# Modulation chunks laid out by outputs and summed by VectorE's accumulator, with the S5 sets respaced

## What is computed

```python
c_act = jax.nn.silu(c)
for layer in range(2):
    mod = (c_act @ ada_w[layer] + ada_b[layer])[:, None, :]      # 6 x 1024 outputs
    shift_m, scale_m, gate_m, shift_f, scale_f, gate_f = jnp.split(mod, 6, axis=-1)
    h = _rmsnorm(x, norm_g[layer, 0]) * (1.0 + scale_m) + shift_m
    mix = _mixer_conv_retention(h, ...) if layer == 0 else _mixer_s5(h, ...)
    x = x + gate_m * mix
    h = _rmsnorm(x, norm_g[layer, 1]) * (1.0 + scale_f) + shift_f
    x = x + gate_f * (jnp.square(jax.nn.relu(h @ w_fc1[layer])) @ w_fc2[layer])
x = _rmsnorm(x, norm_f)
```

## Time and profile before

| | us |
|---|---|
| median of 3 runs | 1222.62 (1221.12 to 1224.0) |
| profiled execution, its own time | 1223.91 |
| its span, first to last instruction | 1222.1 |
| busy: TensorE / VectorE / ACT / POOL | 1181.8 / 856.5 / 531.9 / 434.5 |
| mean granted TensorE clock | 0.989 of full |

### The profile page before, as it was taken

How to read it: one execution, slowest core, us unless ns; L and a number is a source line. 1 busy time by engine, 2 the same in 40 slices (tenths; PEclk the granted TensorE clock), 3 DMA queues, 4 the chain that set the end, 5 groups by cost and what they waited for, 6 DMA issues and landing times.

```text
span 1222.1 us, 24460 instructions
## 1 busy us (share of the span) xinstructions
PE 1181.8 (97%) x10684; PEld 1113.0 (91%) x10684; DVE 856.5 (70%) x953; ACT 531.9 (44%) x675; POOL 434.5 (36%) x575
## 2 busy tenths in 40 slices
PE   6899999999999987999999999999999999999998
PEld 5786788999899977999999999898889999999998
DVE  5699898877679489847896343758885566666633
ACT  2130243543234254436454333466488535444331
POOL 7999689999989526400000001000000031000000
PEclk9899999999999999999999999999999999999999
DMA  9982777988887565374655455444333454545541
GB/s 346 395 329 104 243 257 263 360 301 324 324 313 269 213 234 194 119 256 152 233 181 188 159 205 181 160 143 145 132 136 129 151 182 164 195 154 203 190 159 66
DMA packets 112122, 258.18 MB, mean 211 GB/s; under 512 B 5120, under 2 KB 8848, under 8 KB 111888
## 3 DMA queue, kind: packets, MB, share of 16 engines
q1 hardware_dynamic: 83056, 196.18, 45.1%
q10 hardware_dynamic: 25504, 46.81, 10.8%
q0 software_dynamic: 3456, 13.63, 2.9%
HBM read 241.93 MB, written 14.68 MB: 210 GB/s over the span
## 4 chain that ended last, share of the span: by engine, by line
PE 69%; POOL 15%; issue 2%; DVE 1%; ACT 0%; DMA 0%; DVEq 0%; POOLq 0%
PE bank L1987 69%; POOL tabw L741 6%; POOL tabw L738 3%; POOL prep L746 3%; POOL tabw L746 1%; POOL tabw L777 1%; POOL tabw L779 0%; DMA prep<-in_s_bc 0%; POOL tabw L758 0%; PE bank L2560 0%; POOL s_wout L794 0%; DVE h_in L1408 0%; POOL memory_kv L774 0%; ACT prep L1076 0%; ACT ada_slot_split L919 0%
## 5 line engine op out<-in xcount | busy, mean ns | idle before, releaser
L1987 PE MATMUL bank<-squares_split,ring_split 128*128 128x256 f32 x1056 | 299.4, 284 | 0.0
L1987 PEld LDWEIGHTS bank<-squares_split,ring_split 128*128 128x128 f32 x1056 | 203.4, 193 | 0.0
L1380 DVE SCALAR_TENSOR_TENSOR ada_acc<-ada_slot,cact,ada_acc 128x512 f32<-128x512 f32 x150 | 134.8, 899 | 5.1
L1987 PE MATMUL bank<-ada_slot_split,ring_split 128*128 128x256 f32 x432 | 122.3, 283 | 0.0
L1432 DVE TENSOR_TENSOR ring_split<-ring,ada_slot_split 128x2048 fp32r<-128x2048 f32 (+1 forms) x31 | 70.1, 2264 | 55.8 <-ACT ada_slot_split L919 55.8
L1987 PE MATMUL bank<-big_split,ring_split 128*128 128x256 f32 x352 | 99.5, 283 | 0.0
L831 POOL TENSOR_TENSOR y_cat<-y_cat,tmp 128x512 f32<-128x512 f32 x8 | 10.7, 1339 | 235.8 <-DVE tmp L1891 235.8
L817 POOL TENSOR_TENSOR squares<-squares 128x512 f32<-128x512 f32 x4 | 5.5, 1384 | 240.7 <-ACT squares L1137 194.5
L1987 PE MATMUL bank<-big_split,ada_slot_split 128*128 128x256 f32 x296 | 84.9, 287 | 0.0
L1987 PEld LDWEIGHTS bank<-ada_slot_split,ring_split 128*128 128x128 f32 x432 | 82.9, 192 | 0.0
L1432 DVE TENSOR_TENSOR ring_split<-ring,tabw_split 128x2048 fp32r<-128x2048 f32 x22 | 50.4, 2291 | 41.3 <-ACT tabw_split L919 41.3
(11 more groups left out here) (440 smaller groups left out, 3865.6 us busy)
## 6 DMA issues: line engine op xcount, KB each, us to landing
ring<-in_w_fc SPq DMA_DIRECT2D x32, 2048.0 KB, 8.8
ada_slot<-in_ada_w ACTq DMA_DIRECT2D x20, 2048.0 KB, 11.3
ring<-in_w_in SPq DMA_DIRECT2D x18, 2048.0 KB, 8.3
ring<-in_w_ffn_gate SPq DMA_DIRECT2D x5, 2048.0 KB, 7.9
ring<-in_w_ffn_up SPq DMA_DIRECT2D x5, 2048.0 KB, 7.8
ring<-in_w_ffn_down SPq DMA_DIRECT2D x5, 2048.0 KB, 7.9
ring<-in_w_out SPq DMA_DIRECT2D x4, 2048.0 KB, 8.2
ring<-in_w_branch SPq DMA_DIRECT2D x3, 2048.0 KB, 8.0
```

The source lines that it names most:

```text
L1380: stt(acc, w[:, slab, :], cact[:, slab:slab + 1], acc, ALU.mult, ALU.add)\
L1987: return pe.matmul(*args, skip_group_check=True, **kw)
```

## The change

1. **Chunks by outputs.** The weights are laid out on the host so that a chunk is four tiles of 128 outputs (partitions) by 1024 inputs, 16 KB in one run per partition instead of eight of 2 KB. TensorE's new `condition()` (eight products of the broadcast conditions with the identity) and two copies on VectorE give all partitions the 1024 conditions (`cond`, the former `ada_acc`). VectorE multiplies a tile by them in one instruction of 1024 elements, whose accumulator writes the sum into the column of `mod`; after four tiles it adds the bias.
2. **No `ada(k)` on TensorE for chunks 4 to 23.** Of chunks 0 to 2 TensorE takes one tile, of chunk 3 two (eight one-column products a tile, weights laid out for that).
3. **Sets respaced** by the tables below; `wt1` moves from ahead of the first feed-forward to behind its block 1, `wt7` stands in the middle of the last row block (where `kl7` was) and `kl7` behind `mms`. ACT's copies move with them.
4. **First S5 inputs.** POOL issues the load of set 0's inputs right behind the store of table 6, and waits only for the stores of even tables; ACT waits for the odd ones at its first `s5_weights_out`.
5. **VectorE's order.** `ada_acc(5)` is split in halves, with the four score products between them (they were behind it); the sum of the lag blocks with the skip term moves from ahead of the layer's residual to behind the copies of `uu`; `ada_mod(k)` is gone for k of 4 and more.
6. **ACT's order.** `negate(0)` and `negate(1)` move behind the copies of `uu`, beside `negate(2)`. Waits for `ada21` become waits for `f2.0.3`.
7. `ident` is loaded second on SP's queue, ahead of the chunks. The loads of chunks 4 and 5 and of the panel `q` also wait for the chunk's sums.

```diff
-WT_AFTER = {4: 2, 9: 3, 13: 4}
-KL_AFTER = {2: 1, 7: 2, 11: 3, 15: 4}
-SIDE_ADA = {0: 15, 1: 16, 2: 17, 3: 18, 4: 19, 5: 20}
-SIDE_WT = {1: 5, 3: 6, 5: 7}
-SIDE_KL = {2: 5, 4: 6}
+WT_AFTER = {1: 1, 5: 2, 11: 3}
+KL_AFTER = {3: 1, 8: 2, 14: 3}
+SIDE_WT = {0: 4, 2: 5, 5: 6}
+SIDE_KL = {1: 4, 3: 5, 6: 6}
...
-    jobs += ["f2.0.0", "f2.0.1", "kl7", "f2.0.2", "f2.0.3", "ada21", "ms2", "mms"]
+    jobs += ["f2.0.0", "f2.0.1", "wt7.0", "wt7.1", "f2.0.2", "f2.0.3", "ms2", "mms", "kl7"]
...
-            return a["ada_w"][l][:, 512 * c:512 * c + 512].rearrange("(k p) c -> p k c", p=P)
+            return a["ada_w"][l, c].rearrange("p (i c) -> p i c", i=4)
...
+                if k == 6:
+                    pool.wait_ge(s("s5_scal"), 1)
+                    pool.dma_start(bc[0], a["s5_bc"][0]).then_inc(s("bc_in0"), 16)
...
-            for i in range(2):
-                pool.wait_ge(s(f"tab_out{i}"), 16 * 4)
-            pool.wait_ge(s("s5_scal"), 1)
-            pool.dma_start(bc[0], a["s5_bc"][0]).then_inc(s("bc_in0"), 16)
+            pool.wait_ge(s("tab_out0"), 16 * 4)
...
+                for place, i in tiles[first:end]:
+                    if place > 1 and k < EARLY_ADA:
                         dve.wait_ge(*ada_in(k))
+                    m = 4 * k + i
+                    dot = stt(w[:, place, :], w[:, place, :], 1.0, cond[:, :], ALU.mult, ALU.mult, accum_out=mod[:, m:m + 1])
+                if end == 4:
+                    dot.then_inc(s("ada_acc"), 1)
+                if k >= EARLY_ADA and end == 4:
+                    dve.wait_ge(s("ada_acc"), k + 1)
+                    own = mod[:, 4 * k:4 * k + 4]
+                    tt(own, own, col("ada_b", 4 * k, 4), ALU.add).then_inc(s("mod"), 1)
...
-            ada_acc(5)
+            ada_acc(5, 0, 2)
             for hd in range(4):
                 job_wait(dve, f"sc{hd}")
                 tt(sd[:, hd], ps2(f"sc{hd}"), dtab[:, hd], ALU.mult).then_inc(s("sd"), 1)
+            ada_acc(5, 2)
             ada_acc(6)
...
-            negate(2)
+            for k in range(3):
+                negate(k)
             act.wait_ge(s("wout_out"), 16 * 8)
...
+            def condition():
+
+                pe.wait_ge(s("cact"), 1)
+                pe.wait_ge(s("ident_in"), 16)
+                for k in range(KT):
+                    last = mm(bank[6 + k // 4][:, P * (k % 4):P * (k % 4) + P], cact[:, k:k + 1].broadcast_to([P, P]), ident[:, :],
+                              start=True, stop=True)
+                last.then_inc(s("cond"), 1)
```

More of the change, by code:

```diff
@@ L44 @@
 KEEP_BUSY = {}
-DVE_SLABS = 6
-PE_SLABS = {k: (0, 1) if k == EARLY_ADA - 1 else (6, 7) for k in range(EARLY_ADA)}
+PE_TILES = (((0, 3),),) * 3 + (((0, 3), (2, 2)),)
+DVE_TILES = (((1, 0), (2, 1), (3, 2)),) * 3 + (((1, 0), (3, 1)),)
 COLS = {}
@@ L137 @@
 BANKS = 6
-LATE_WEIGHTS = ("wt5.0", "wt5.1", "kl5", "wt6.0", "wt6.1", "kl6", "wt7.0", "wt7.1", "kl7")
+LATE_WEIGHTS = ("wt4.0", "wt4.1", "kl4", "wt5.0", "wt5.1", "kl5", "wt6.0", "wt6.1", "kl6", "wt7.0", "wt7.1", "kl7")
 DRIVES = 5
@@ L645, in _ @@
                     job_wait(sp, "ada3")
+                    sp.wait_ge(s("ada_acc"), 4)
                 if name == "av":
@@ L1059, in decay_row @@
                                    scale=mag4[:, 4 * n + q:4 * n + q + 1]).then_inc(s("decay"), 1)
-            job_wait(act, "ada21")
-            for k in range(2):
-                negate(k)
+            job_wait(act, "f2.0.3")
             decay_row(0)
@@ L1066, in _ @@
             root("mms")
+            s5_lags_out(7)
             for n in (1, 2):
@@ new lines, in condition, with ada_acc @@
+            def condition():
+                dve.wait_ge(s("cond"), 1)
+                for i in range(2):
+                    dve.tensor_copy(cond[:, 512 * i:512 * i + 512], bank[6 + i][:, :]).then_inc(s("cond"), 1)
+            def ada_acc(k, first=0, end=4):
+                tiles = DVE_TILES[k] if k < EARLY_ADA else [(i, i) for i in range(4)]
+                w = ada_slot(k)
+                if k == 0:
+                    dve.wait_ge(s("cond"), 3)
+                if k < EARLY_ADA:
+                    dve.wait_ge(s(f"first_half{k}"), 16)
+                elif first == 0:
+                    dve.wait_ge(*ada_in(k))
+                for place, i in tiles[first:end]:
+                    if place > 1 and k < EARLY_ADA:
+                        dve.wait_ge(*ada_in(k))
+                    m = 4 * k + i
[6 more added lines that the diff above has]
+                    tt(own, own, col("ada_b", 4 * k, 4), ALU.add).then_inc(s("mod"), 1)
@@ L1383, in ada_mod @@
             def ada_mod(k):
+                dve.wait_ge(s("ada_acc"), k + 1)
+                n = len(DVE_TILES[k])
+                own = mod[:, 4 * k:4 * k + n]
+                tt(own, own, col("ada_b", 4 * k, n), ALU.add)
                 job_wait(dve, f"ada{k}")
-                tt(mod[:, 4 * k:4 * k + 4], ps(f"ada{k}")[:, 0:4], col("ada_b", 4 * k, 4), ALU.add).then_inc(s("mod"), 1)
+                tt(mod[:, 4 * k + n:4 * k + 4], ps(f"ada{k}")[:, n:4], col("ada_b", 4 * k + n, 4 - n), ALU.add).then_inc(s("mod"), 1)
@@ L1577, in _ @@
                     split_low(j + 3)
-                if j in ADA_AFTER and j < 15:
-                    ada_mod(ADA_AFTER[j])
                 if j in ADA_HALVES:
                     k, half = ADA_HALVES[j]
-                    ada_acc(k, 4 * half, 4 * half + 4)
-            ada_mod(14)
+                    ada_acc(k, 2 * half, 2 * half + 2)
             ada_acc(16)
@@ L1944, in begin @@
                     k = int(name[3:])
-                    if 2 <= k < EARLY_ADA:
+                    if k >= 2:
                         pe.wait_ge(s("mod"), k - 1)
-                    elif k >= EARLY_ADA:
-                        pe.wait_ge(s("mod"), k)
-                elif name in ("wt5.0", "wt5.1"):
-                    before = TURN["mms" if name == "wt5.1" else "ms2"] - BANKS
+                elif name in ("wt4.0", "wt4.1"):
+                    before = TURN["mms" if name == "wt4.1" else "ms2"] - BANKS
                     pe.wait_ge(s(freed[ROTATING[before]][0]), freed[ROTATING[before]][1])
-                elif name in ("kl5", "kl6", "kl7"):
+                elif name in ("kl4", "kl5", "kl6", "kl7"):
                     pe.wait_ge(s("klc"), int(name[2]))
```

167 lines of the change are left out of this document (60 added, 107 removed), and 3 rows, old and new, of the table jobs.

## The result

The changed kernel takes 1230.24 us (median of 4 runs, 1228.56 to 1231.59), the kernel before on the same chip 1223.31. The ratio is 1.0057, 95% interval 1.0036 to 1.0078. The profiled execution has a span of 1228.6 us and an own time of 1230.39, 6.5 us above before's.

What follows compares the result with a forecast made beforehand. TensorE, busy for 97% of the span, was taken as the bound, with VectorE pacing the S5 stage. Gains of 3.1 + 1.6 - 0.7 = 4.0 us gave 1219.9 for the profiled execution, 1218.6 as median, range 1207 to 1229.

Steps and rivals of the forecast that it cites:

- the fourth part: Behind the last S5 set: store, loads, negate(2), dd copies and TensorE's jobs take 30.7 us to drive 4, ending at 450.7.
- the last set: POOL's S5 sets: c7 ends at 420, range 412 to 429, with c5 waiting for kl4 until 329.1.
- rival B: VectorE's long products hold POOL back more than the free end returns: c7 at 424 to 430, 1222 to 1229; chance 0.20.
- VectorE sets the pace: S5 stage: VectorE's directions follow without idle time, 3.66 us each; TensorE waits, and direction 4's earlier start gains 3.1 us.
- half clock priced at 0.7: TensorE ahead of outputs 0: a longer wait can bring a clock dip of up to 1.7 us; 0.7 was taken.
- the start: Kernel start: less work after the chunks' last landing lets TensorE start 2.65 us sooner, and q0 3.4 us sooner.
- g0: Gate projection: ACT's copies wait behind a chunk load, the gap grows to some 4.8 us, and only 1.4 of 3.4 us stay.
- rival D: Longer chunk packets delay the weight panels, so the start's gain is lost at q: 1220 to 1225; chance 0.08.
- The product itself: VectorE's chunk products: 1.35 us for 1024 elements, so a chunk costs 5.5 us instead of 6.95.
- Rival C: VectorE's accumulating product runs at half rate, 2.4 us each and 9.6 us a chunk: 1235 or more; chance 0.07.
- POOL's early start: Before the S5 sets: with first inputs issued earlier, POOL starts near 144, 11 us sooner, a gain lost again at set 2.
- After the S5 stage: Second feed-forward: chunks 22 and 23 leave TensorE, saving 1.6 us.

Runs made afterwards that it cites:

- run 6: The changed kernel with ACT's loads of chunks 4 and 5 held until the panel ag has landed: 1225.42 us, ratio 1.0037 to before.
- run 3: The changed kernel with each product of 1024 in chunks 4 to 23 cut into two of 512: 1224.13 us, ratio 1.0016 to before.
- run 1: The changed kernel with SP loading table 2 behind wout2, ahead of win3 and panel ga0: 1224.84 us, ratio 1.0040 to before.
- run 7: The changed kernel with ACT's copies of va ahead of its load of chunk 7: 1226.25 us, ratio 1.0036 to before.

## Why the prediction was wrong

It forecast 1218.6, faster, with a range to 1229. Measured are 1230.24. The chain of the fourth part (last set, table 2, negate(2), dd copies, drive 4) was the one that decided, and the last set came where rival B put it, between 424 and 430, on the slow side of 423.1; B had 0.20 and the forecast 0.50. But B's own price at 424.5 gives 1223.1 (455.2 at drive 4, 1.4 us later, less 1.6, plus 0.7), 7 us short. So the last set is the smaller part of the miss. **What failed is the stretch behind it: "VectorE sets the pace" in the S5 stage, 30.7 us from the last set to drive 4, and half clock priced at 0.7.** The trace of run 6 is a check: there the last set is stored at 420.2, where I had forecast it, but drive 4 ends at 453.9 and not at 450.7, and z7 at 509.4, before at 509.2. The S5 stage gains nothing. That trace is of its fastest execution (1222.34, median 1225.42).

- **The last set, 420 forecast, 424.5 measured: the number near, the mechanism wrong.** 3.0 of the 4.5 us is the start of set 2 (214.1 against 211.1), which comes from the start and g0, below. The six sets then took 210.3 us against 208.9, and this agreement is luck. I let POOL wait for kl4 (329.1) and charged the longer products only to the chunks beside c5 to c7. In the trace kl4 (332.1) held nothing: POOL had no wait, and c5's first product came at 341.99 because its own operations were slower. From set 2's start to there POOL took 127.9 us, before 110.9; behind it 82.5 us against the 89.8 of the sum, since x7 and c7, with no chunks beside them, took 20.5 us and not 33.6. In the changed kernel's second execution the two parts are 121.2 and 88.3 us, so only their sum (210.3 and 209.5) is firm. Without waits the sets took 200.7 before. So POOL's operations grew by some 9 us where I had "nothing net", of which short products give 7.6 back (run 3), and the wait for kl4 that I had instead did not come.
- **TensorE's own list, not priced.** I wrote that the jobs on TensorE come some ten microseconds sooner at the S5 stage and that kl5 would be through before POOL asks. It was the other way round: TensorE stood 10.67 us for c5 at kl5 and ended f2.0.3 no sooner than before. VectorE finished direction 3 at 452.4. So even with drive 4 at 450.7 direction 4 could have gained 1.4 us and not 3.1.
- **From the last set to drive 4, 30.7 forecast, 34.2 measured.** Of the 3.5 us, 0.9 is the table's landing, 25.4 us behind the set's store instead of 24.5: SP waited for kl7, which the change had put behind mms, from 428.1 to 429.92, and a part of that was made up on the queue. I had written that kl7's new place costs nothing. 2.7 is the half clock: outputs 0 and drive 4 took 6.2 us at 0.52 and 3.5 at 1.00 (run 1). I had 0.7 for that, "mostly in VectorE's shadow"; there is no shadow, because VectorE itself waits for drive 4.
- **Inside the S5 stage: not forecast, 3.3 us.** VectorE waited 6.2 us for drives behind direction 4, before 3.0. I had read VectorE as the pace there, so that time before direction 4 would pass on one to one. Counted from drive 4 to z7 it looks different: 57.8 us before and 58.8 changed (57.1 in its second execution). Before, drive 4 was done 2.3 us ahead of VectorE, and that lead went into the later drives; in the changed kernel it is gone. So 2.3 of the 3.3 us is the lead lost and 1.0 lies within the spread: over all fourteen traces z7 follows drive 4 by 55.5 to 61.1 us. This reading is argued from the traces; no run isolates it, and what makes the spread stays open. The largest of these waits in the changed kernel (timeline, VectorE):

```profile
470.51 0.69 DVE L1623 TENSOR_TENSOR big<-bank,tabw 128x512 f32<-128x512 f32 x1 [0.73 <-PE bank L1975]
...
479.24 0.69 DVE L1623 TENSOR_TENSOR big<-bank,tabw 128x512 f32<-128x512 f32 x1 [1.32 <-PE bank L1975]
...
484.71 0.69 DVE L1623 TENSOR_TENSOR big<-bank,memory_kv 128x512 f32<-128x512 f32 x1 [1.73 <-PE bank L1975]
```

- **The start, 2.65 us forecast, 1.0 measured, and 3.4 at q0, measured -0.7.** I took the chunk's sums for the end of that chain. It ends with av's panel: ACT waits for its second half (landed at 34.7, before at 35.6), then issues chunk 4's load, then makes TensorE's first input (timeline, ACT):

```profile
34.72 0.38 ACTq L587 DMA_DIRECT2D ada_slot<-in_ada_w  x1
35.20 1.70 ACT L867 ACTIVATE h_in<-h_in,mod 128x256 f32<-128x256 f32 x4 [15.11 <-DVE h_in L1414]
```

  VectorE had begun its part of the norm at 33.19, so it was ACT that came late, and TensorE's gap was 3.17 us. av0 then took 10.2 us instead of 9.0; the granted clock was 0.50 from 38 to 42 us, before 0.67. That spent the 1.0 us, ag0 took 1.4 longer by the late panel, and chunk 4's sums, gone from ahead of q0, gave 0.9 back. That was rival D (0.08), true for the ag panel rather than for q. It is not an alternative to B; it adds to it, and my rivals were built as if only one could hold.
- **g0.** 4.8 us of gap forecast, 4.2 measured. The gap was right; that more than half of it passes on is what run 7's trace says.
- **The product itself.** 1.35 us forecast; the answer to the earlier trace rows is the line's own view (durations min/median/max in ns):

```profile
L1373 DVE SCALAR_TENSOR_TENSOR ada_slot<-ada_slot,ada_acc x86: 1212/1413/1761, 9.3 to 631.3; 128x1024 f32<-128x1024 f32 x86
L1373 DVE DVE_READ_ACCUMULATOR ada_slot<-ada_slot,ada_acc x86: 76/77/86, 10.5 to 632.4; 128x1 f32 x86
```

It takes 1212 ns when no POOL work stands beside it, plus 76 for reading the accumulator; beside POOL's operations it is longer, and the mean of the 86 is 1447 ns. So a chunk costs VectorE 6.1 us and not 5.5. The rule of the Trainium skill, "Vector Engine (DVE) Microarchitecture Reference", section 7, that this operation halves its throughput with two such sources, is not borne out: half of the rate seen without accumulator would put it above 2 us, and the longest of 86 was 1.76. The measurement decides. Rival C fell.
- **POOL's early start.** 144 forecast, 150.1 measured: the tables, computed beside the same long products, ended 6.1 us later. With short products it is 148.6, with the old chunks 144.4. So the length of the products explains 1.5 us of it, and the rest stays open.
- **After the S5 stage.** 1.6 us forecast, 1.7 measured.

Up to direction 4 the errors sum to 8.0 us (4.5 for the set, 3.5 for the tail), with 3.3 behind it. Less the 0.7 that the forecast had for the clock, and 0.1 behind the stage, that is 10.5 us, the whole way from the 1219.9 forecast for the profiled execution to its 1230.39. The other 1.1 of the 11.6 us is no mechanism: I set the median 1.3 us below the profiled execution, and it was 0.15 below.

## What to carry to other kernels

Before an engine's short instructions are merged into long ones, look at which engine works beside them and is slowed by each: here the other engine got through by the instruction, not by the microsecond, and it was the one that ended last. A gain on the busiest engine brings forward only what is not held by another chain, so follow each chain to its end with the new durations in every stage, not only in the one where it was last seen waiting. A load with longer runs can hold up the loads beside it, and a load stuck behind a weight panel on its queue can be the last link of a chain of computation.

## What the runs showed of the hardware

- A POOL operation beside a long two-source VectorE instruction ended when that one did: 2.72 us beside one of 2.53, 0.63 alone. Cutting the same work into twice as many instructions gave POOL 7.6 us in 210, and brought its operations above 1.2 us from 72 to 30.
- The accumulating product showed no price for the accumulator in its rate: 1212 ns for 1024 elements, both sources in SBUF, where a subtraction of 2048 took 2298; reading the accumulator took 76 ns.
- The 2 MB loads of chunks 4 and 5, in runs of 16 KB, held up a load that had been queued 20 us earlier on another queue, by about 7.5 us (47.1 against 39.6).
- Behind a gap of 7.2 us TensorE's granted clock was 0.50 over the next 6 us; behind one of 1.5 us it was 1.00. The same 120 products took 6.2 and 3.5 us, 2.7 us on a path that waits for them.
